# One feed-forward norm and two norms between blocks applied after the products, with per-tile operands, VectorE residual adds and one product for the bias rows

## What is computed

```
# first block, end
x = x + gate_m * (... @ w_out)                          # "out"
h = rmsnorm(x, norm_mlp_w) * (1 + scale_f) + shift_f    # "n1"
x = x + gate_f * (square(relu(h @ w_up)) @ w_down)      # "up0","down0","up1","down1"
x = rmsnorm(x, norm_final_w)                            # "n2"
# second block, start
h = concat(meta_tokens, x)
h = h + dsa_attention(rms_norm(h, ln_attn_g), w_in_a, ...)   # "n3", product "ia"
bias = rel_table[rel_bucket(key_pos - query_pos)]       # 8 heads, shape 528 x 528 each
```

## Time and profile before

| what | value |
|---|---|
| median of 3 runs | 2648.97 us (2642.8 to 2652.46) |
| the profiled execution | 2647.37 us, its span 2645.5 us |
| TensorE matmul busy | 2453.2 us, 93% of the span |
| VectorE, ScalarE, GpSimd busy | 1371.2, 1057.0, 483.1 us |
| chain that ended last | TensorE 78%, VectorE 9%, ScalarE 5%, issue 4%, DMA 3%, GpSimd 2% |
| granted TensorE clock, mean | 0.944 of full speed |

### The profile page before, as it was taken

How to read it: one execution, slowest core, us unless ns; L and a number is a source line. 1 busy time by engine, 2 the same in 40 slices (tenths; PEclk the granted TensorE clock), 3 DMA queues, 4 the chain that set the end, 5 groups by cost and what they waited for, 6 DMA issues and landing times.

```text
span 2645.5 us, 39964 instructions
## 1 busy us (share of the span) xinstructions
PE 2453.2 (93%) x14683; PEld 2135.7 (81%) x14683; DVE 1371.2 (52%) x2002; ACT 1057.0 (40%) x1905; POOL 483.1 (18%) x416
## 2 busy tenths in 40 slices
PE   5899888999879999978998999999999989999998
PEld 4678766887757878857776999999978859999987
DVE  5886566423444314345773576663333344666631
ACT  5545554433423223222444433332355543333322
POOL 0000434611460000351012221210100001211200
PEclk8998889999989989978999999999999968999999
DMA  7463322332323333322210233333422211333232
GB/s 273 139 212 104 84 76 50 94 96 73 101 65 87 95 108 99 95 64 88 59 49 17 80 88 93 88 89 91 118 65 65 58 49 48 88 87 95 85 96 89
DMA packets 409222, 238.29 MB, mean 90 GB/s; under 512 B 11186, under 2 KB 400149, under 8 KB 409125
## 3 DMA queue, kind: packets, MB, share of 16 engines
q1 hardware_dynamic: 400325, 202.24, 27.4%
q0 software_dynamic: 8192, 32.59, 3.4%
q10 hardware_dynamic: 608, 2.16, 0.2%
HBM read 231.84 MB, written 4.98 MB: 90 GB/s over the span
## 4 chain that ended last, share of the span: by engine, by line
PE 78%; DVE 9%; ACT 5%; issue 4%; DMA 3%; POOL 2%; SPq 0%; POOLq 0%; DVEq 0%; ACTq 0%
PE PS L490 58%; PE PS L1989 5%; PE PS L1778 3%; DMA w_raw<-in_w_in_dram 1%; DVE ada_acc L636 1%; PE PS L1725 1%; PE PS L2025 1%; PE PS L2061 1%; PE PS L1793 1%; ACT w_hi L415 1%; PE PS L1857 1%; PE PS L2063 1%; DVE conv_acc L2187 1%; DVE z L2281 1%; PE PS L1893 1%
## 5 line engine op out<-in xcount | busy, mean ns | idle before, releaser
L421 DVE TENSOR_TENSOR w_lo<-w_raw,w_hi 128x1024 fp32r<-128x1024 f32 (+1 forms) x368 | 481.7, 1309 | 710.3 <-ACT w_hi L415 709.4
L490 PE MATMUL PS<-op_hi,w_hi 128*128 128x264 f32 (+2 forms) x2264 | 633.6, 330 | 32.8 <-DVE op_lo L568 10.9
L490 PE MATMUL PS<-op_lo,w_hi 128*128 128x264 f32 (+2 forms) x2264 | 630.1, 329 | 0.0
L490 PE MATMUL PS<-op_hi,w_lo 128*128 128x264 f32 (+2 forms) x2264 | 628.6, 328 | 0.0
L415 ACT ACTIVATE w_hi<-w_raw 128x1024 fp32r<-128x1024 f32 (+1 forms) x368 | 380.9, 1035 | 239.5 <-PE PS L490 206.7
L490 PEld LDWEIGHTS PS<-op_hi,w_hi 128*128 128x128 f32 (+1 forms) x2264 | 382.7, 189 | 85.3 <-issue 20.7
L490 PEld LDWEIGHTS PS<-op_hi,w_lo 128*128 128x128 f32 (+1 forms) x2264 | 381.6, 189 | 38.8 <-issue 1.3
L490 PEld LDWEIGHTS PS<-op_lo,w_hi 128*128 128x128 f32 (+1 forms) x2264 | 380.9, 189 | 37.8 <-issue 1.7
L490 PE MATMUL PS<-ff_hi,w_lo 128*128 128x512 f32 (+1 forms) x784 | 240.3, 343 | 0.0
L490 PE MATMUL PS<-ff_hi,w_hi 128*128 128x512 f32 (+1 forms) x784 | 239.9, 342 | 0.0
L490 PE MATMUL PS<-ff_lo,w_hi 128*128 128x512 f32 (+1 forms) x784 | 239.9, 342 | 0.0
(11 more groups left out here) (455 smaller groups left out, 3923.2 us busy)
## 6 DMA issues: line engine op xcount, KB each, us to landing
w_raw<-in_w_up_dram SPq DMA_DIRECT2D x120, 512.0 KB, 3.8
w_raw<-in_w_in_dram SPq DMA_DIRECT2D x64, 512.0 KB, 4.0
w_raw<-in_w_down_dram SPq DMA_DIRECT2D x64, 512.0 KB, 3.9
w_ada<-in_w_ada_dram POOLq DMA_DIRECT2D x12, 2048.0 KB, 10.1
decay<-sums_scratch SPq DMA_DIRECT2D x16, 512.0 KB, 5.3
w_raw<-in_w_branch_ssd_dram SPq DMA_DIRECT2D x16, 512.0 KB, 3.9
w_raw<-in_w_in_a_dram SPq DMA_DIRECT2D x16, 512.0 KB, 3.9
w_raw<-in_w_kv_b_dram SPq DMA_DIRECT2D x16, 512.0 KB, 3.8
```

The source lines that it names most:

```text
L421: dve.tensor_tensor(wlo[slot][:, 0:ks, :], wraw[slot][:, 0:ks, :], whi[slot][:, 0:ks, :].bitcast(F32), ALU.subtract).then_inc(sem("w_split ...
L490: last = pe.matmul(a[0:l.cols, h, 0:cn], w[slot][:, k, 0:l.cols], x[:, kk, c0:c0 + cn], start=(j == 0 and k == 0 and w is whi and x is l.h ...
```

## The change

Norm n1 is applied late: VectorE adds each "out" group to the residual, with its gate, out of PSUM (`gated_add`); the operands of "up0" and "up1" are the residual times a gain per channel, made tile by tile, without the reciprocal. The shift cannot be scaled by the reciprocal, so it stands in two more columns ahead of the tokens (`META - 2`), and each group of "up0" and "up1" becomes products of 258 and 256 columns in two banks. VectorE multiplies a finished group by the reciprocal and copies the shift's result to a column that is the bias of ScalarE's relu. TensorE's sum for n1 stands inside group 0 of "up0", ahead of input tile 6.

Norms n2 and n3 are merged. The operands of "ia" are residual times `norm_final_w` times `ln_attn_g`. Two sums of squares are kept, one plain (GpSimd, in `square`) and one weighted by `norm_final_w` squared plus a small term (VectorE, in `sumsq`), and both are summed on TensorE after group 1 of "ia". The residual itself is scaled by n2's reciprocal in groups 2 to 4 of "ia". The mixed branches get buffers of their own (`MXh`, `MXl`, with 512 columns a tile), since `HH` and `HL` now are written while "out" reads its operands. The bias rows are one product with the whole table as weights, giving 8 partitions, one per head; the write to HBM repeats each of them 128 times.

```diff
+        MXh = at("mixed_hi", [P, KD, S], F32R, A_S + KD * S * 4)
+        MXl = at("mixed_lo", [P, KD, S], F32R, F + KD * S * 4)
...
-        brow = at("bias_rows", [P, QH, ROWL], F32, F + 65536)
+        brow = at("bias_rows", [QH, ROWL], F32, F + 65536)
...
+            L[f"up{half}"].shift = True
...
+        def acc_shift(l, par):
+            flat = acc_of(l, par).rearrange("p a n -> p (a n)")
+            return flat[:, 0:1], flat[:, 2:1022].rearrange("p (a n) -> p a n", a=2)[:, :, 0:S // 2]
...
+            if l.shift:
+                cols = [(META - 2, S // 2 + 2), (META + S // 2, S // 2)]
...
+                    if mid and k == KD - 2:
+                        mid()
...
+        def resid_tile_hi(act, name, l, gain, g, c0=0):
             s0 = SUMS[name][0]
             act.wait_ge(sem("evacuated"), l.G0 + g + 3)
-            act.activation(HH[:, g, :], R[:, g, :], ACT.Copy, scale=gain(g)).then_inc(sem("norm_hi"), 1)
+            act.activation(HH[:, g, c0:T], R[:, g, c0:T], ACT.Copy, scale=gain(g)).then_inc(sem("norm_hi"), 1)
             if g >= 3:
                 act.wait_ge(sem("sumsq_ready"), s0 + g - 2)
-            act.activation((sacc if g == 0 else et[g % 2])[:, :], R[:, g, :], ACT.Square).then_inc(sem("resid_sq"), 1)
-        def resid_hi(act, name, l, gain):
-            evac_loop(act, l, lambda g, t, par: resid_tile_hi(act, name, l, gain, g), first=KD)
+            act.activation((sacc if g == 0 else et[g % 2])[:, c0:T], R[:, g, c0:T], ACT.Square).then_inc(
+                sem("resid_sq"), 1)
...
+        def gated_add(dve, l, g, t, par, gate):
+            r = R[:, g, META:T]
+            dve.wait_ge(sem("units_done"), unit_of(l, t, par, l.upg - 1) + 1)
+            dve.scalar_tensor_tensor(r, acc_view(l, par), modc[:, gate + g:gate + g + 1], r, ALU.mult, ALU.add).then_inc(
+                sem("evacuated"), 1)
...
-            resid_add(pool, link, "out", L["out"], 0)
+            resid_sum(pool, "n1", META)
...
-            pool.wait_ge(sem("bias_rows"), QH)
-            pool.dma_start(scratch[:, :, 0:REL], brow[:, :, 0:REL]).then_inc(sem("bias_out"), 16)
-            resid_add(pool, link, "down1", L["down1"], 8)
-            pool.wait_ge(sem("norm_sum"), 2)
-            link(pool.memset(sacc[:, :], 0.0))
-            for k in range(KD):
-                pool.wait_ge(sem("x_normed"), k + 1)
-                link(pool.tensor_tensor(sqt[:, :], R[:, k, :], R[:, k, :], ALU.mult))
-                pool.tensor_tensor(sacc[:, :], sacc[:, :], sqt[:, :], ALU.add).then_inc(sem("sumsq_ready"), 1)
-                pool.wait_ge(sem("sumsq_ready"), 16 + k + 1)
+            resid_add(pool, "down0", L["down0"])
+            pool.wait_ge(sem("bias_rows"), 1)
+            pool.dma_start(scratch.rearrange("p h n -> h p n")[:, :, 0:REL],
+                           brow[:, 0:REL].unsqueeze(1).to_broadcast([QH, P, REL])).then_inc(sem("bias_out"), 16)
+            s0, q0 = SUMS["n2"]
+            for g in range(KD):
+                pool.wait_ge(sem("resid_sq"), q0 + g + 1)
+                if g == 0:
+                    pool.tensor_copy(sqt[:, :], et[0][:, :]).then_inc(sem("sumsq_ready"), 1)
+                else:
+                    pool.tensor_tensor(sqt[:, :], sqt[:, :], et[g % 2][:, :], ALU.add).then_inc(sem("sumsq_ready"), 1)
+                pool.wait_ge(sem("sumsq_ready"), s0 + g + 1)
...
+            act.activation(HH[:, :, META - 2:META], modc[:, 24:32].unsqueeze(2).to_broadcast([P, KD, 2]), ACT.Copy)
+            resid_hi(act, "n1", L["out"], mlp_gain, META)
...
-                def relu(g, t, par, l=L[f"up{half}"], name=f"up{half}"):
-                    act.wait_ge(sem(name + "_sq"), t * 2 + par + 1)
-                    act.activation(et[par][:, 0:S], acc_view(l, par), ACT.Relu).then_inc(sem("evacuated"), 1)
-                def sq_hi(g, t, par, name=f"up{half}"):
+                def relu_hi(g, t, par, l=L[f"up{half}"], name=f"up{half}"):
+                    evacuated(act, l, t, par)
+                    act.activation(et[par][:, 0:S], et[par][:, 0:S], ACT.Relu, bias=small[:, 6 + par:7 + par]).then_inc(
+                        sem(name + "_relu"), 1)
                     act.wait_ge(sem(name + "_sq"), t * 2 + par + 3)
                     act.activation(tile_of(FH, g), vt[par][:, 0:S], ACT.Copy).then_inc(sem(name + "_hi"), 1)
-                evac_loop(act, L[f"up{half}"], relu, sq_hi)
-                resid_evac(act, f"down{half}", L[f"down{half}"], 40)
+                evac_loop(act, L[f"up{half}"], lambda g, t, par: None, relu_hi)
...
-                    for h in range(QH):
-                        act.wait_ge(sem("bias_ps"), h + 1)
-                        b = 4 + 2 * (h % 2)
-                        act.activation(brow[:, h, 0:512], bank(b), ACT.Copy)
-                        act.activation(brow[:, h, 512:REL], bank(b + 1)[:, 0:REL - 512], ACT.Copy).then_inc(
-                            sem("bias_rows"), 1)
-            norm_root(act, "n2", META, EPS1)
-            gained_hi(act, "n3", attn_gain, HH, ("x_normed", 1))
+                    act.wait_ge(sem("bias_ps"), 1)
+                    act.activation(brow[:, 0:512], bank(4)[0:QH, :], ACT.Copy)
+                    act.activation(brow[:, 512:REL], bank(5)[0:QH, 0:REL - 512], ACT.Copy).then_inc(
+                        sem("bias_rows"), 1)
...
+            def final_hi(g, t, par):
+                l = L["down1"]
+                act.wait_ge(sem("evacuated"), l.G0 + g + 3)
+                if g == 0:
+                    act.wait_ge(sem("meta_v"), 1)
+                    act.activation(HH[:, :, 0:META], vt[0][:, 0:P].rearrange("p (k m) -> p k m", k=KD), ACT.Copy)
+                act.activation(HH[:, g, META:T], R[:, g, META:T], ACT.Copy, scale=final_gain(g)).then_inc(
+                    sem("norm_hi"), 1)
+                if g >= 2:
+                    act.wait_ge(sem("sumsq_ready"), SUMS["n2"][0] + g - 1)
+                    act.wait_ge(sem("weighted"), g - 1)
+                act.activation(et[g % 2][:, :], R[:, g, :], ACT.Square).then_inc(sem("resid_sq"), 1)
+            evac_loop(act, L["down1"], final_hi, first=KD)
...
-            norm_sum(pe, "n1", META, 8)
-            products(pe, L["up0"], "n1_ready")
+            products(pe, L["up0"], "n1_ready", mid=lambda: norm_sum(pe, "n1", META, 7))
...
-            for h in range(QH):
-                if h >= 2:
-                    pe.wait_ge(sem("bias_rows"), h - 1)
-                b = 4 + 2 * (h % 2)
-                lhs = tab[:, h:h + 1].to_broadcast([32, P])
-                pe.matmul(bank(b), lhs, oh[:, 0:512], start=True, stop=True)
-                pe.matmul(bank(b + 1)[:, 0:REL - 512], lhs, oh[:, 512:REL], start=True, stop=True).then_inc(
-                    sem("bias_ps"), 1)
+            pe.matmul(bank(4)[0:QH, :], tab[:], oh[:, 0:512], start=True, stop=True)
+            pe.matmul(bank(5)[0:QH, 0:REL - 512], tab[:], oh[:, 512:REL], start=True, stop=True).then_inc(
+                sem("bias_ps"), 1)
             products(pe, L["up1"], None)
             products(pe, L["down1"], "up1_ready")
-            pe.wait_ge(sem("bias_rows"), QH)
-            norm_sum(pe, "n2", META, 16)
...
-                    pe.wait_ge(sem("sumsq_ready"), 24)
+                    pe.wait_ge(sem("weighted"), KD + 1)
...
+                    pe.wait_ge(sem("sumsq_ready"), SUMS["n2"][0] + KD)
+                    pe.matmul(bank(7), ones, sqt[:, META:T], start=True, stop=True).then_inc(sem("norm_sum"), 1)
...
-            post_loop(dve, L["out"])
-            norm_rows(dve, link, "n1", META, lambda k: aff[:, 8 + k:9 + k], lambda k: modc[:, 24 + k:25 + k], HH, HL,
-                      True)
+            def out_lo(g, t, par):
+                gated_add(dve, L["out"], g, t, par, 16)
+                dve.wait_ge(sem("norm_hi"), g + 1)
+                if g == 0:
+                    dve.tensor_tensor(HL[:, :, META - 2:META], modc[:, 24:32].unsqueeze(2).to_broadcast([P, KD, 2]),
+                                      HH[:, :, META - 2:META].bitcast(F32), ALU.subtract)
+                dve.scalar_tensor_tensor(HL[:, g, META:T], R[:, g, META:T], mlp_gain(g), HH[:, g, META:T].bitcast(F32),
+                                         ALU.mult, ALU.subtract).then_inc(sem("norm_ready"), 1)
+            post_loop(dve, L["out"], out_lo, first=KD)
...
+                def scale(g, t, par, name=name):
+                    l = L[name]
+                    dve.wait_ge(sem("units_done"), unit_of(l, t, par, 0) + 1)
+                    dve.wait_ge(sem(name + "_sq"), t * 2 + par + 1)
+                    shift, x = acc_shift(l, par)
+                    dve.tensor_copy(small[:, 6 + par:7 + par], shift)
+                    dve.tensor_tensor(halves(et[par][:, 0:S]), x, halves(rs[:, META:T]), ALU.mult).then_inc(
+                        sem("evacuated"), 1)
+                def square_lo(g, t, par, name=name):
...
-            dve.wait_ge(sem("norm_std"), 2)
-            link(dve.reciprocal(rs[:, META:T], rs[:, META:T]))
```

(54 more changed lines are left out.)

121 lines of the change are left out of this document (44 added, 77 removed).

## The result

The changed kernel takes 2619.18 us (2615.58 to 2625.33, 4 runs) against 2649.82 us: ratio 0.9891, 95% interval 0.9867 to 0.9915. It is faster by 31 us, where 66.5 were forecast. The measured time is 37 us above the forecast of 2582.5 us; rival A gave 2616.

What follows compares the result with a forecast made beforehand. The prediction took TensorE, the chain that ended last for 78% of the span, as the bound. Its terms summed to -66.5 us, from 2647.4 to 2580.9, with the median forecast at 2582.5 us and the range 2574 to 2624.

Steps and rivals of the forecast that it cites:

- rival A: Bias-row write from 8 partitions starves "up1" of weights: 33 us lost by the middle, 2616 us; chance 0.35.
- Step 8: Write of the bias rows to HBM, now from 8 partitions: taken as hidden, 0 us; write bounds 8.9 and 142 us.
- the likeliest case: Whole kernel, all terms as summed with the bias-row write hidden: 2582.5 us, own range 2574 to 2593; chance 0.48.
- B: Bias-row write at a full sixteenth of the rate, 142 us, starves all of "up1": 2705 us, slower; chance 0.06.
- C: Per-group chains of VectorE and ScalarE in "up0" and "up1" not hidden: 22 us lost, 2605 us; chance 0.07.
- D: Stages behind "ia", index scores and selection, swallow 15 of the 32 us gained there: 2598 us; chance 0.04.
- Step 1: Between "out" and "up0": group 0 of "up0" runs as soon as "out" ends, saving 22.6 us.
- 2, "out" itself: In "out": operands move to tiles of 512 columns, making its eight groups faster, saving 1.1 us.
- 3, groups of "up0" and "up1": Groups become 48 products, 5.71 us each instead of 5.58: costs 4.0 us, bounds 0 and 8.7.
- 4, bias rows: Ahead of "up1": one pair of products, and "up1" follows at once: saves 17.0 us, bounds 15.4 and 17.
- step 5: From "down1" to group 2 of "ia": 15.9 us instead of 47.9, saving 32.0 us.
- Step 6: Ahead of `ki_wi`: VectorE's reciprocal and eight scalings in groups 2 to 4 of "ia" cost 2.2 us, bounds 0 and 5.

Runs made afterwards that it cites:

- the two other places: Changed kernel with the eight bias rows in every fourth partition of 32, or every sixteenth of 128: 2584.27 us and 2595.95 us, one run each.
- the kernel with 128 partitions: Changed kernel with bias rows on all 128 partitions, each written 8 times, and the read back adapted: 2581.46 us, ratio 0.9735 to the kernel before.

## Why the prediction was wrong

Step 8 is the one that failed: "I take it as hidden still, by the nearest row, the same bytes at 8.9 us". The nearest row was near in bytes and far in partitions. Measured: 55.4 us, and 40 us of TensorE with the clock behind the gap.

Choosing between the case and rival A, I gave A 0.35, though the only rows against it were the loads of "ia" that got through beside a read into all 128 partitions; none showed a transfer from so few. Rival A was right in mechanism and place. That it is so near in time, 2616 us for 2619, is in part luck: its loss of 33 us was 40, and the rest of the kernel came out some 3 us faster than the sum. The stated range of 2574 to 2624 holds 2619 only because it was drawn to take in A; the likeliest case's own range ended at 2593.

The engines do take packets by turns, as A said, but a turn of the write is 5.2 KB and not 2.6, so a load gets an eleventh of the bytes and not a sixth, and the turns start late. So no load that the changed kernel issued into the running write landed before its end, where A let one or two through. Rival A also names "a queue shared with the loads"; the write is on GpSimd's queue and the loads on SyncE's, and what they share is the engines. The estimate that the prediction worked out from the Trainium skill, "SBUF — State Buffer", section "Door 1: The DMA port swizzle", was 49 us for the write; the measured 55.4, with the two other places, bears its rule out. B's full sixteenth did not come. C and D fell: the chains per group show 5.73 us, and the gain at "ia" was kept.

By steps, forecast and measured, in us:

| step | forecast | measured |
|---|---|---|
| 1, "out" to "up0" | -22.6 | -22.7 |
| 2, "out" itself | -1.1 | -1.1 (5.44 a group) |
| 3, groups of "up0" and "up1" | +4.0 (5.71 a group) | +4.6 (5.73) |
| 4, bias rows | -17.0 | -17.1 |
| 5, "down1" to "ia" | -32.0 | -31.5 |
| 6, ahead of `ki_wi` | +2.2 | +0.8 |
| 8, the write | 0 | +40 |

Step 1's thin cover held. In step 5 the 0.9 us of issue was missing. Step 6 was right about VectorE, which scales `ki_wi` 2.3 us later counted from group 2, and wrong about the end: the scores start 1206.38 - 1180.19 = 26.2 us after group 2 instead of 1234.47 - 1209.12 = 25.35, because the later copy took 2.2 us and not 3.7. The steps without 8 add up to -67, and the kernel with 128 partitions took 70 off, interval 63 to 78. With step 8 they give -27 where 31 were measured; the 4 us between are within the interval of the first result (23 to 35) and were not traced.
